# Nine whole slots for the expert matrices, and the expert results weighted by slot and brought back through a plain one-hot matrix in two rounded parts

## What is computed

```python
# second_block, after its attention
h2 = modulate(rmsnorm(x, g_ffn), shift_ffn, scale_ffn)            # (256, 1024)
# top-1 of 4 groups, then top-2 of its 8 experts; weights: group gate x share
def expert_block(xb, e):                                          # xb: the tokens of expert e
    return (silu(xb @ w_gate[e]) * (xb @ w_up[e])) @ w_down[e]    # 1024 -> 512 -> 1024
y = zeros; y[token] += weight * expert_block(...)                 # two experts per token
x = x + gate_ffn * y
return rmsnorm(x, g_final)
```

## Time and profile before

| | us |
|---|---|
| median of 3 runs | 1098.78 |
| lowest and highest | 1098.1, 1101.7 |
| the profiled execution | 1095.0 |
| its span, from the first to the last instruction | 1093.2 |

### The profile page before, as it was taken

One profiled execution on the slowest core, in us unless ns is written; L12 is line 12 of the kernel. 1 busy time (PEld: TensorE's weight loads), 2 busy tenths in 40 slices (PEclk: granted clock), 3 DMA queues, 4 the chain that ended last, 5 costly groups with the idle time before them and its releaser, 6 DMA issues.

```text
span 1093.2 us, 15144 instructions
## 1 busy us (share of the span) xinstructions
PE 1016.3 (93%) x5951; PEld 706.6 (65%) x5951; DVE 538.4 (49%) x901; ACT 330.3 (30%) x507; POOL 75.3 (7%) x109
## 2 busy tenths in 40 slices
PE   6798689999999999999988899999999999999995
PEld 5697569999899998889876444444444444433441
DVE  6756786988989996738674311111111011111113
ACT  4353645445445455527450100000000000000001
POOL 7200010110111110100010000000000000000000
PEclk9899689999999999899989999999999999999998
DMA  7315046778898864244345899799999999999991
GB/s 279 116 40 195 37 155 231 265 275 300 300 330 280 302 242 164 78 160 149 126 170 230 355 425 382 314 384 426 426 425 431 421 426 427 423 426 430 426 401 40
DMA packets 60366, 311.88 MB, mean 285 GB/s; under 512 B 4021, under 2 KB 5386, under 8 KB 47530
## 3 DMA queue, kind: packets, MB, share of 16 engines
q1 hardware_dynamic: 52464, 284.31, 66.1%
q0 software_dynamic: 7456, 26.91, 6.7%
q10 hardware_dynamic: 410, 0.16, 0.1%
HBM read 310.32 MB, written 1.05 MB: 285 GB/s over the span
## 4 chain that ended last, share of the span: by engine, by line
PE 78%; DVE 10%; DMA 5%; ACT 3%; issue 2%; SPq 0%; POOL 0%; DVEq 0%; POOLq 0%; ACTq 0%
PE bank L1134 10%; PE bank L1103 10%; PE bank L744 10%; PE bank L1094 10%; PE bank L745 10%; PE bank L746 10%; PE bank L1045 6%; PE bank L1058 5%; DVE ring_r L1516 5%; DMA ring<-in_w_up 3%; DMA ring<-in_w_in 2%; PE bank L829 1%; PE bank L798 1%; ACT ring_r L1203 1%; DMA final_g<-in_w_ada 1%
## 5 line engine op out<-in xcount | busy, mean ns | idle before, releaser
L744 PE MATMUL bank<-hT_r,ring_r 128*128 128x256 f32 x744 | 217.0, 292 | 11.9 <-DVE ring_r L1516 8.3
L746 PE MATMUL bank<-hT_r,ring_r 128*128 128x256 f32 x744 | 213.8, 287 | 0.0
L1516 DVE TENSOR_TENSOR ring_r<-ring,ring_r 128x2048 fp32r<-128x2048 f32 (+1 forms) x78 | 176.1, 2290 | 21.5 <-ACT ring_r L1203 21.0
L1203 ACT ACTIVATE ring_r<-ring 128x2048 fp32r<-128x2048 f32 (+1 forms) x78 | 144.1, 1891 | 46.0 <-DMA ring<-in_w_up 38.8
L744 PEld LDWEIGHTS bank<-hT_r,ring_r 128*128 128x128 f32 x744 | 146.4, 197 | 15.4 <-issue 9.9
L746 PEld LDWEIGHTS bank<-hT_r,ring_r 128*128 128x128 f32 x744 | 146.2, 197 | 0.0
L745 PE MATMUL bank<-v_tok_r,ring_r 128*128 128x256 f32 x512 | 145.5, 284 | 0.0
L1980 DVE TENSOR_TENSOR scratch<-scratch,bank 128x512 f32<-128x512 f32 x16 | 11.0, 687 | 237.0 <-PE bank L1103 237.0
L1103 PE MATMUL bank<-ring,scratch 128*64 128x512 f32 x496 | 113.3, 595 | 0.0
L1134 PE MATMUL bank<-ring,scratch 128*64 128x512 f32 x480 | 106.3, 595 | 6.6 <-ACT scratch L1417 6.6
L1094 PE MATMUL bank<-ring,scratch 128*64 128x512 f32 x480 | 105.6, 592 | 0.0
(11 more groups left out here) (292 smaller groups left out, 1417.8 us busy)
## 6 DMA issues: line engine op xcount, KB each, us to landing
ring<-in_w_up SPq DMA_DIRECT2D x47, 2048.0 KB, 12.6
ring<-in_w_down SPq DMA_DIRECT2D x37, 2048.0 KB, 10.3
ring<-in_w_gate SPq DMA_DIRECT2D x30, 2048.0 KB, 12.1
ring<-in_w_in SPq DMA_DIRECT2D x9, 2048.0 KB, 8.0
kT<-in_w_ada POOLq DMA_DIRECT2D x24, 512.0 KB, 9.1
ring<-in_w_out SPq DMA_DIRECT2D x4, 2048.0 KB, 8.3
scratch<-in_w_ada POOLq DMA_DIRECT2D x12, 512.0 KB, 6.5
final_g<-in_w_ada POOLq DMA_DIRECT2D x12, 512.0 KB, 7.1
```

The source lines that it names most:

```text
L744: pe.matmul(dst, lhs[0], rhs[0], start=start, stop=False, **flags)
L746: return pe.matmul(dst, lhs[1], rhs[0], start=False, stop=stop, **flags)
L1203: sc.activation(hi, raw, ACT.Copy).then_inc(s_whi, 1)
L1516: last = ve.tensor_tensor(lo, raw, hi, ALU.subtract)
```

## The change

Four things, all in the expert stage.

1. The tensors are laid out so that kT with v_tok, bias with post_attn, and hT with mix follow the ring without a gap, as three more slots of 2 MB. A view `eslots` sees 9 slots. The 96 matrices go through them in order: matrix m of the sequence gate, gate, up, up, down, down of each pair takes slot `ESLOTS[m % 9]`. The waits in front of the loads are one matrix apart, not two. Two places differ early on: the third slot outside the ring, bias with post_attn, is now filled after the last use of post_attn, and the first extra slot now takes an up matrix of pair 0.
2. As 9 slots and 6 matrices per pair meet again every 3 pairs, the loops of SP and TensorE hold three pairs in a turn (`PERIOD`): TensorE has pairs 0 to 2 written out, then four turns of three, then pair 15. The loops of ScalarE and VectorE keep one pair.
3. `combT` becomes a plain one-hot matrix (VectorE compares the transposed `onehw` with zero), rounded to fp32r, and a sum over the same row gives each slot its weight (`wslot`).
4. `ye` has two parts of 1024 columns, both fp32r: ScalarE writes the weighted result, rounded, half by half (`ye[:, 0]`); VectorE writes the weighted result less that (`ye[:, 1]`). `combine` multiplies both parts with the one-hot matrix: 8 matmuls in fp32r in place of 4 in f32. Before, ScalarE and VectorE each copied one half of the columns, side by side; now each goes over both, VectorE behind ScalarE.

```diff
+    ESLOT_N = 9
+    ESLOTS = (0, 3, 6, 1, 4, 2, 5, 7, 8)
+    PERIOD = 3
...
-        combT = piece(T, P)
-        ye = piece(D)
+        combT = piece(T, P, of=scratch_r)
+        ye = piece(2, D, of=scratch_r)
+        wslot = piece(1)
...
+        eslots = nc.alloc_sbuf_tensor_at("eslots", [P, ESLOT_N, SLOT_W], f32, offset=places["ring"])
...
+        def expert_slot(u, c, e):
+
+            return ESLOTS[(6 * u + 2 * c + e) % ESLOT_N]
...
+            def pair_loads(p, u, last_one=False):
+
+                into(expert_slot(u, 0, 0), matrix(0, 2 * p), (s_eu, p - 1))
+                into(expert_slot(u, 0, 1), matrix(0, 2 * p + 1), (s_edn, p - 1))
+                into(expert_slot(u, 1, 0), matrix(1, 2 * p), None)
+                into(expert_slot(u, 1, 1), matrix(1, 2 * p + 1), (s_eg, p))
+                into(expert_slot(u, 2, 0), matrix(2, 2 * p), None)
+                if not last_one:
+                    into(expert_slot(u, 2, 1), matrix(2, 2 * p + 1), (s_eu, p))
+
+            into(0, matrix(0, 0), consumed(N_MOE - LANES))
+            into(LANES, matrix(0, 1), None)
+            into(SLOT_N, matrix(1, 0), (s_src["mix2"], T))
+            into(1, matrix(1, 1), consumed(N_MOE - LANES + 1))
+            into(LANES + 1, matrix(2, 0), None)
+            into(2, matrix(2, 1), consumed(N_MOE - LANES + 2))
+            into(LANES + 2, matrix(0, 2), None)
+            into(SLOT_N + 1, matrix(0, 3), (s_src["moe"], T))
+            into(SLOT_N + 2, matrix(1, 2), (s_back, 4))
+            into(expert_slot(1, 1, 1), matrix(1, 3), (s_eg, 1))
+            into(expert_slot(1, 2, 0), matrix(2, 2), None)
+            into(expert_slot(1, 2, 1), matrix(2, 3), (s_eu, 1))
+            pair_loads(2, 2)
+            with sp.Fori(1, PAIRS // PERIOD) as r:
+                for u in range(PERIOD):
+                    pair_loads(PERIOD * r + u, u)
+            pair_loads(PAIRS - 1, PAIRS - 1, last_one=True)
...
             def combine(p, bank_done=None):
 
                 pe.wait_ge(s_combT, p + 2)
-                pe.wait_ge(s_yA, p + 2)
                 pe.wait_ge(s_yV, p + 2)
                 for t in range(T):
                     for c in range(2):
-                        last = pe.matmul(ACC[2 * t + c][:, :], combT[:, t, :], ye[:, c * HALF:(c + 1) * HALF],
-                                         start=False, stop=False, skip_group_check=True)
+                        for part in range(2):
+                            last = pe.matmul(ACC[2 * t + c][:, :], combT[:, t, :],
+                                             ye[:, part, c * HALF:(c + 1) * HALF], start=False, stop=False,
+                                             skip_group_check=True)
...
-            pair(0)
-            pair(1)
-            pair(2)
-            with pe.Fori(3, PAIRS - 1) as p:
-                pair(p)
-            pair(PAIRS - 1, last_one=True)
+            for u in range(PERIOD):
+                pair(u, u)
+            with pe.Fori(1, PAIRS // PERIOD) as r:
+                for u in range(PERIOD):
+                    pair(PERIOD * r + u, u, r)
+            pair(PAIRS - 1, PAIRS - 1, last_one=True)
...
+                sc.wait_ge(s_combT, p + 2)
                 sc.wait_ge(s_edn, p + 1)
-                sc.activation(ye[:, 0:HALF], PS[4][:, :], ACT.Copy).then_inc(s_yA, 1)
+                for c in range(2):
+                    sc.activation(ye[:, 0, c * HALF:(c + 1) * HALF], PS[4 + c][:, :], ACT.Copy, scale=wslot)\
+                        .then_inc(s_yhi, 1)
...
-                ve.tensor_copy(combT, PS[7][:, 0:S].rearrange("p (t n) -> p t n", t=T)).then_inc(s_combT, 1)
-                ve.wait_ge(s_edn, p + 1)
-                ve.tensor_copy(ye[:, HALF:D], PS[5][:, :]).then_inc(s_yV, 1)
+                ve.tensor_scalar(combT, PS[7][:, 0:S].rearrange("p (t n) -> p t n", t=T), 0.0, None, ALU.not_equal)
+                ve.tensor_reduce(wslot, PS[7][:, 0:S], X, ALU.add).then_inc(s_combT, 1)
+                ve.wait_ge(s_combT, p + 2)
+                for c in range(2):
+                    half = slice(c * HALF, (c + 1) * HALF)
+                    ve.wait_ge(s_yhi, 2 * p + c + 1)
+                    last = ve.scalar_tensor_tensor(ye[:, 1, half], PS[4 + c][:, :], wslot, ye[:, 0, half], ALU.mult,
+                                                   ALU.subtract)
+                last.then_inc(s_yV, 1)
```

More of the change, by code:

```diff
@@ L188, in two_block_kernel, with piece @@
         off = [0]
-        def piece(*shape):
+        scratch_r = rounded_view("scratch", [P, 7168])
+        def piece(*shape, of=scratch):
             n = int(np.prod(shape))
-            v = scratch[:, off[0]:off[0] + n]
+            v = of[:, off[0]:off[0] + n]
             off[0] += n
@@ L216, in two_block_kernel @@
         cmax, over = piece(1), piece(1)
[L218 to L226, removed]
-        softplus = lambda n: junk[:, n % 2 * HALF:n % 2 * HALF + 384]
[L229 to L235, removed]
+        assert off[0] <= 7168
+        eslots = nc.alloc_sbuf_tensor_at("eslots", [P, ESLOT_N, SLOT_W], f32, offset=places["ring"])
+        for n, (low_half, high_half) in enumerate((("kT", "v_tok"), ("bias", "post_attn"), ("hT", "mix"))):
+            assert places[low_half] == places["ring"] + 4 * SLOT_W * (SLOT_N + n)
+            assert places[low_half] < places[high_half] < places[low_half] + 4 * SLOT_W
+        assert places["x_tok"] == places["ring"] + 4 * SLOT_W * ESLOT_N
+        softplus = lambda n: junk[:, n % 2 * HALF:n % 2 * HALF + 384]
         SB_ADD = bias[:, 8:10, :].rearrange("p a s -> p (a s)")[:, 0:384]
@@ L246, in two_block_kernel @@
         R_C, R_PRE, R_FPRE, R_MIX, R_FFN, R_SWA, R_DIL, R_SB, R_SUB = 0, 8, 16, 24, 32, 40, 44, 48, 52
-        loaded = [sem(f"loaded{i}") for i in range(SLOT_N)]
+        loaded = [sem(f"loaded{i}") for i in range(ESLOT_N)]
         s_x = [sem(f"s_x{t}") for t in range(T)]
@@ L432, in consumed, with expert_turn, later_slot, later_turn @@
             return s_proj[1], 2 * (T - 1) + n - N_OUT2 + 1
-        def expert_slot(c, e):
+        def expert_slot(u, c, e):
+            return ESLOTS[(6 * u + 2 * c + e) % ESLOT_N]
+        def expert_turn(u, c, e):
+            before_experts = N_MOE // LANES if expert_slot(u, c, e) < LANES else 0
+            return before_experts + (6 * u + 2 * c + e) // ESLOT_N + 1
+        def later_slot(c, e):
             return c + LANES * e
-        def expert_loads(c, e):
-            return 0 if e else N_MOE // LANES
+        def later_turn(c, e):
+            slot = later_slot(c, e)
+            used = sum(ESLOTS[m % ESLOT_N] == slot for m in range(6 * PAIRS))
+            return (N_MOE // LANES if slot < LANES else 0) + used + 1
         KA = (0, 5)
@@ L565, in _ @@
                 straight(N_OUT2 + c, w_out2[:, :, c * HALF:(c + 1) * HALF])
[L567 to L578, removed]
@@ L592, in _ @@
[L592 to L605, removed]
@@ L606, in _ @@
[L606 to L615, removed]
@@ L616, in _, with matrix, into @@
-            dst = ring[:, expert_slot(2, 1), :].rearrange("p (k n) -> p k n", k=KE)
-            for half, done in enumerate((s_half, loaded[expert_slot(2, 1)])):
+            def matrix(c, n):
+                return (w_gate, w_eup, w_edown)[c][:, ds(n, 1), :, :].rearrange("p o k n -> p (o k) n")
+            def into(slot, src, free):
+                if free is not None:
+                    sp.wait_ge(*free)
+                dst = eslots[:, slot, :].rearrange("p (k n) -> p k n", k=src.shape[1])
+                sp.dma_start(dst, src).then_inc(loaded[slot], 16)
@@ L618, in _ @@
+            dst = eslots[:, slot, :].rearrange("p (k n) -> p k n", k=KE)
+            sp.wait_ge(s_eu, PAIRS - 1)
+            for half, done in enumerate((s_half, loaded[slot])):
                 tiles = slice(half * KE // 2, (half + 1) * KE // 2)
@@ L622, in _ @@
             with sp.If(n_pairs > PAIRS):
+                sp.wait_ge(s_edn, PAIRS)
                 with sp.Fori(1, PASSES) as r:
                     with sp.Fori(0, PAIRS) as q:
-                        for c, done in enumerate((s_eg, s_eu, s_edn)):
-                            expert_load(r * PAIRS + q, q, c, (done, r * PAIRS + q))
+                        for c, used in enumerate((s_eg, s_eu, s_edn)):
+                            sp.wait_ge(used, r * PAIRS + q)
+                            for e in range(2):
+                                into(later_slot(c, e), matrix(c, 2 * q + e), None)
             rows = out.rearrange("o (t p) d -> p (o t) d", p=P)
@@ L1153, in _ @@
                 with pe.Fori(PAIRS, PAIRS * PASSES) as p:
-                    pair(p)
+                    pair(p, None)
             combine(n_pairs - 1, bank_done=s_comb_last)
```

49 lines of the change are left out of this document (18 added, 31 removed).

## The result

The changed kernel took 1079.13 us (median of 4 runs, 1077.59 to 1080.35), the kernel before 1099.2 us beside it (4 runs, 1098.1 to 1101.7): a ratio of 0.9823, with a 95% interval of 0.9803 to 0.9843. The prediction said 1079.3 us. The profiled execution took 1080.35 us, its span 1078.7 us.

What follows compares the result with a forecast made beforehand. TensorE set the end, with loads barely keeping up. Combine's saving, capped by the loads at 20.5 us, less 1.0 at the end, gave 19.5 us: 1098.8 - 19.5 = 1079.3 us, range 1071 to 1088.

Steps and rivals of the forecast that it cites:

- Combine, 3.63 to 2.02 us: TensorE's combine in each pair: 8 fp32r matmuls at 0.227 us plus 0.2 us, saving 1.61 us per pair.
- D: Rival, chance 0.08: combine's rounded matmuls do not overlap, 3.3 us per combine, 4 us saved in all, 1095 us.
- TensorE's limit: Expert stage: 15 combines ahead of the last down save 1.61 us each, 24.2 us, or 23.2 after the end's cost.
- The loads' limit: Expert stage: 83 more matrices after the 11th cap the saving, 18.8 us at 4.92 us each, 19.5 taken at 4.91.
- A: The forecast itself, chance 0.45: loads bind in the last few pairs of the expert stage, 1076.5 to 1082 us.
- C: Rival, chance 0.15: loads run slower than today's mean, 5.0 us per matrix, losing 6.6 us: 1086 us.
- The slots alone: Three more load slots in the expert stage: give nothing by themselves, but decide how much of combine's saving is kept.
- VectorE and ScalarE in the loop at nothing: Expert loop: slot weights lie under down, the result's second half under the next gate, so they cost nothing.
- The end, +1.0 us: Last pair, where no gate follows: combine starts 1.4 us later, its first bank takes 0.4 us less, +1.0 in all.
- E: Rival, chance 0.10: TensorE's threefold loop body is fetched anew each turn; at 3 us per fetch, 1127 us.
- The base: Starting time of the forecast: saving taken off the median, 1098.8 us, not off the profiled execution, 1095.0 us.

Runs made afterwards that it cites:

- fewer bytes: Changed kernel with half of the second down matrix of pairs 2 to 14 not loaded (13.6 MB less): 1075.12 us, repeat 1077.62 us.
- half a combine: Changed kernel multiplying only the rounded parts in combine, 4 fp32r matmuls per pair in place of 8: 1079.88 us, ratio 0.9798 to the kernel before.
- Without the slots: Kernel before with the new fp32r combine but its six-slot ring and order of loads: 1085.08 us, ratio 0.986 to the kernel before.

## Why the prediction was right, step by step

- **Combine, 3.63 to 2.02 us:** measured 2.03. The overlap of the output projection's rounded matmuls carried over, and D fell. Fifteen combines are 24.0 us.
- **TensorE's limit, 24.2 us of the stage:** 22.9 by the run with fewer bytes. Of the 24.0 us of the fifteen combines the middle pairs of the four turns take back 0.73; 0.3 us is not assigned.
- **The loads' limit:** I had 83 matrices at 4.91 us. At 428 GB/s they take 4.90 each. Up of pair 15 starts 427.39 us after the first gate; my 1042.9 us for the 94th matrix at 4.92 us is 428.5 us after the first gate of the profile that it was worked out from, and 426.8 at 4.90. From that up to the eviction it is 16.40 us, 16.35 before.
- **Who binds:** A held, by less than I wrote. I expected pairs of 29.4 us after pair 12; instead the three waits come at pairs 14 and 15 and hold 1.63 us. Both limits lie 2.0 us apart, as the runs with half a combine (nothing gained) and fewer bytes (2.0 us gained) show from either side; my sums had 3.7 (24.2 against 20.5 off the stage). C, loads at 5.0 us, has no row in its favour.
- **The slots alone are worth nothing and decide how much is kept:** both held. The queue had indeed run dry before, most of all from 700 to 725 us (294 GB/s), a stretch that the prediction's rows leave out. Without the slots the stage keeps 11.8 us of the saving instead of 21.0. The share that this makes in the median is open.
- **VectorE and ScalarE in the loop at nothing:** the comparison took 0.42 and the sum 0.41 us, and TensorE's list has no wait for either beyond the last pair. The copies after down were mis-sized, without an effect in the loop: a scaled and rounded copy took 0.68 us on ScalarE (I had 0.60) and VectorE's operation 0.75 us (I had 0.69).
- **The end, +1.0 us:** +1.14, by those same two durations.
- **E, the loop body:** it stayed resident, and the jumps back cost nothing that the trace shows. What I had at nothing was 0.18 us per turn, ahead of the middle pair's down, also in the three turns without a packet. The Trainium skill (Runtime: NRT & Kernel Launch, Instruction fetch mechanics) warns of a fetch at each taken branch out of the window held and gives 128 KiB for TensorE; the trace agrees with the second, as a body of about 57 KB (my estimate from the earlier trace rows) ran three more turns without a packet.
- **The base:** I took the saving off the median and not off the profiled execution. The second look at the kernel before shows why that was right: the profiled 1095.0 us had reached its first gate 5.4 us earlier than the other execution, with the same stage. That the median came out within 0.2 us of the forecast is luck all the same: the changed kernel's three medians are 1079.13, 1080.08 and 1080.92 us, and its single executions spread from 1076.88 to 1084.21.

## What to carry to other kernels

When two resources are full at once, compute both limits from one anchor (here the 11th matrix and 83 more) and let the tighter one cap the saving; a run that takes work off the one and a run that takes bytes off the other then show the distance between them. Places for loads, with waits one matrix apart, cost next to nothing (0.7 us here, by the threefold loop body) and give nothing as long as the loads are ahead, but they decide how much of a later saving on the compute side is kept, because a queue that once ran dry and is full from then on doesn't get the bytes back. Compare profiles from an event at the start of the changed stage, not from the start of the span.

## What the runs showed of the hardware

- A load queue that always has work moved 428 GB/s for 300 us, 4.90 us per matrix of 2 MB. A matrix then lands a median of 25 us or more after its issue (12 us before), and this costs nothing. The kernel after, its issues from 706 to 1035 us (KB each, median us from issue to landing):

```profile
eslots<-in_w_gate SPq DMA_DIRECT2D x22, 2048.0 KB, 25.1
```

- A loop body of three pairs ran four turns and was fetched once (4 packets in the first turn, none after). The jumps back cost TensorE nothing visible (6.91 to 6.92 us from down to gate, as in straight code). Each turn has one wait that is 0.18 us longer, in its middle pair, which straight code doesn't have; its cause is open.
- Two executions of one program differed by 5.4 us ahead of a stage that took 464.75 us in both. In the window from 569 to 600 us the granted clock was 0.96 in the one and 0.94 in the other, and TensorE was busy 27.67 against 25.51 us.
- Writing fp32r with a scale per partition made a 128x512 copy out of the accumulator 0.68 us on ScalarE, where the plain one took 0.598. The type and the scale changed together, so which of them costs it isn't shown.
- A wait of 0.55 to 0.60 us for a load in TensorE's list lengthened its pair by about 0.7 us (pair 8 without the slots: 1.47 us for two).
